# Self-attention in pairs of heads: four score matmuls in a row, four blocks of transposes, alternating value matmuls, twice the buffers

## The reference, cut to what matters

```python
q = rope(q.reshape(B, S, N_ATTN_HEADS, HEAD_DIM), positions)      # 8 heads of 64
k = rope(k.reshape(B, S, N_ATTN_HEADS, HEAD_DIM), positions)
v = v.reshape(B, S, N_ATTN_HEADS, HEAD_DIM)
attn = dilated_mixture_attention(q, k, v).reshape(B, S, ATTN_WIDTH)
...
h = h + jnp.concatenate([attn, rec], axis=-1) @ w_out[l]
h = h + memory_cross_attention(rmsnorm(h, norm_cross_g[l]), rmsnorm(memf, norm_mem_g[l]),
                               w_cq[l], w_ck[l], w_cv[l], w_co[l])
```

## Time and profile before

| | |
|---|---|
| median of three runs | 2299.41 us |
| span of the profiled execution, first to last instruction | 2294.4 us |
| TensorE busy / VectorE / ScalarE / GpSimd | 2110.9 / 984.3 / 756.1 / 738.7 us |
| mean granted TensorE clock | 0.950 |
| self-attention, first score to the output product | 1697.03 to 1787.97 us |

### The profile page before, as it was taken

One profiled execution on the slowest core, in us unless ns is written; L12 is line 12 of the kernel. 1 busy time (PEld: TensorE's weight loads), 2 busy tenths in 40 slices (PEclk: granted clock), 3 DMA queues, 4 the chain that ended last, 5 costly groups with the idle time before them and its releaser, 6 DMA issues.

```text
span 2294.4 us, 26745 instructions
## 1 busy us (share of the span) xinstructions
PE 2110.9 (92%) x9626; PEld 1668.1 (73%) x9626; DVE 984.3 (43%) x1417; ACT 756.1 (33%) x1049; POOL 738.7 (32%) x323
## 2 busy tenths in 40 slices
PE   6999999999999987688899999979589978999997
PEld 6888888888768763456788888857453656888886
DVE  6733277145436027773511111377836344221224
ACT  2422122111364134342342222445445343332332
POOL 1323233323324211232244344423330312534432
PEclk9999999999999998777999999989789998999999
DMA  7322244234212110000233232322130211323321
GB/s 300 110 101 82 83 166 154 84 119 146 73 57 81 60 50 28 10 1 21 87 94 111 91 103 89 119 63 79 57 100 1 73 37 55 111 89 93 110 83 64
DMA packets 54426, 197.21 MB, mean 86 GB/s; under 512 B 6432, under 2 KB 6992, under 8 KB 53584
## 3 DMA queue, kind: packets, MB, share of 16 engines
q1 hardware_dynamic: 45424, 162.98, 22.5%
q10 hardware_dynamic: 8928, 33.23, 4.1%
HBM read 194.09 MB, written 2.10 MB: 86 GB/s over the span
## 4 chain that ended last, share of the span: by engine, by line
PE 78%; issue 10%; DVE 7%; ACT 3%; POOL 2%; ACTq 0%; POOLq 0%; DVEq 0%; PEldq 0%
PE ps L1518 62%; POOL wlo L443 2%; PE ps L1532 2%; PE ps L1823 2%; PE ps L1832 1%; PE ps L1505 1%; PE ps L1506 1%; PE ps L1507 1%; PE ps L1753 1%; PE ps L1688 1%; PE ps L1681 1%; PE ps L1842 1%; PE ps L1741 1%; PE ps L1729 1%; DVE decay_f L1198 1%
## 5 line engine op out<-in xcount | busy, mean ns | idle before, releaser
L443 POOL TENSOR_TENSOR wlo<-raw,whi 128x1024 fp32r<-128x1024 f32 x280 | 697.5, 2503 | 1433.6 <-ACT whi L474 1433.5
L1518 PE MATMUL ps<-h_hi,whi 128*128 128x512 f32 (+1 forms) x1600 | 520.7, 364 | 13.7 <-POOL wlo L443 6.5
L1518 PE MATMUL ps<-h_lo,whi 128*128 128x512 f32 (+1 forms) x1600 | 522.0, 365 | 0.0
L1518 PE MATMUL ps<-h_hi,wlo 128*128 128x512 f32 (+1 forms) x1600 | 518.5, 363 | 0.0
L474 ACT ACTIVATE whi<-raw 128x1024 fp32r<-128x1024 f32 x280 | 289.5, 1053 | 436.2 <-PE ps L1518 346.1
L1518 PEld LDWEIGHTS ps<-h_hi,whi 128*128 128x128 f32 x1600 | 273.1, 188 | 71.9 <-issue 11.7
L1518 PEld LDWEIGHTS ps<-h_hi,wlo 128*128 128x128 f32 x1600 | 275.6, 189 | 51.2
L1518 PEld LDWEIGHTS ps<-h_lo,whi 128*128 128x128 f32 x1600 | 274.3, 188 | 47.8 <-issue 0.7
L1518 PE MATMUL ps<-g_lo,whi 128*128 128x512 f32 (+1 forms) x784 | 260.4, 369 | 0.0
L1518 PE MATMUL ps<-g_hi,whi 128*128 128x512 f32 (+1 forms) x784 | 258.4, 366 | 0.0
L1518 PE MATMUL ps<-g_hi,wlo 128*128 128x512 f32 (+1 forms) x784 | 258.4, 366 | 0.0
(11 more groups left out here) (332 smaller groups left out, 2422.0 us busy)
## 6 DMA issues: line engine op xcount, KB each, us to landing
raw<-panels SPq DMA_DIRECT2D x280, 512.0 KB, 3.5
ada_w<-ada_t ACTq DMA_DIRECT2D x54, 512.0 KB, 4.3
ada_f<-ada_p SPq DMA_DIRECT2D x9, 512.0 KB, 15.4
ada_f<-ada_t SPq DMA_DIRECT2D x9, 512.0 KB, 15.5
x_lat<-x_t SPq DMA_DIRECT2D x1, 2048.0 KB, 9.6
out<-x_lat SPq DMA_DIRECT2D x8, 256.0 KB, 2.2
cond_b<-cond SPq DMA_DIRECT2D x1, 1024.0 KB, 4.9
x_ctx<-ctx_t SPq DMA_DIRECT2D x1, 1024.0 KB, 11.6
```

Of the source, the lines that this page charges most:

```text
L443: pool.tensor_tensor(wlo[:, sl], raw[:, sl], whi[:, sl].bitcast(f32), ALU.subtract).then_inc(lo_done, 1)
L1518: ins = pe.matmul(bank(banks + b, n), wt[:, w], a[:, at_(kc, c0):at_(kc, c0) + n], start=kc == 0 and j == 0, stop=kc == n_k - 1 and j == 2)
```

## The change

The items of the self-attention are reordered. An item n is now head 2*(n div 8) + n mod 2 and query tile (n div 2) mod 4, so the two heads of a pair alternate. TensorE works in groups of four items (`GROUP`): four score matmuls in a row, then four blocks of transposes of the group before. Every second group, from the fourth on, the value matmuls of a whole pair follow, in which the two heads alternate. ScalarE's copy now lies four items behind its exponential. There are eight probability rows (the second four where `x_ctx` was) and two buffers `prob_t` of a pair each. The cross-attention becomes a function of its own with its old order; its buffers are the new ones.

The diff, cut to its core (the functions for ScalarE and VectorE of the cross-attention keep their order and are left out; `item` and the addresses are shown once):

```diff
-P_BUFS = 4
+P_BUFS = 8
 LAG = 3
+GROUP = 4
...
-        prob = at("prob", P_BUFS * LAT, R_ADA + 8 * KB)
+        prob_a = at("prob_a", P_BUFS // 2 * LAT, R_ADA + 8 * KB)
+        prob_b = at("prob_b", P_BUFS // 2 * LAT, R_XC)
...
-        prob_t = at("prob_t", 2 * LT * LAT, R_H + 32 * KB)
+        prob_t = [at("prob_t0", 2 * LT * LAT, R_H + 32 * KB), at("prob_t1", 2 * LT * LAT, R_G + 24 * KB)]
...
+        def item(A, n):
+            if A is SELF:
+                j, it, e = n // 8, n // 2 % LT, n % 2
+                return 2 * j + e, it
+            return divmod(n, LT)
...
+            def self_attention():      # ScalarE
+                for n in range(SELF["n"] + GROUP):
+                    if n < SELF["n"]:
+                        exponential(SELF, n)
+                    if n >= GROUP:
+                        m = n - GROUP
+                        if m % 8 == 0 and m >= 16:
+                            act.wait_ge(a_values, m // 4 - 2)
+                        transposed(SELF, m)
+                        if m % 8 == 5 and m > 8:
+                            merged(SELF, m // 8 - 1)
+                merged(SELF, HEADS - 1)
...
+                    if A is SELF and n % 8 == 6 and n >= 16:      # VectorE
+                        low_output(A, n // 8 - 2)
...
+            def scores(A, n):      # TensorE
+                hd, it = item(A, n)
+                j, r = (hd // 2, slice(64 * (hd % 2), 64 * (hd % 2) + 64)) if A is SELF else (hd, slice(0, P))
+                if n >= 4:
+                    pe.wait_ge(a_max if A is SELF else a_exp, A["n0"] + n - 3)
+                pe.matmul(bank(SCORE_BANKS[n % 4], A["keys"]), A["q"][r, j * LAT + it * P:j * LAT + (it + 1) * P],
+                          A["k"][r, j * A["keys"]:(j + 1) * A["keys"]], start=True, stop=True).then_inc(a_scores, 1)
+            def transposes(A, m):
+                N = A["n0"] + m
+                pe.wait_ge(a_prob, N + 1)
+                if m >= 2:
+                    pe.wait_ge(a_copied, N - 1)
+                for t in range(A["keys"] // P):
+                    ins = pe.transpose(bank(2 + m % 2, P, t * P), prob_row(N, P, t * P), ident[:, :])
+                ins.then_inc(a_trans, 1)
+            def self_attention():
+                pe.wait_ge(win2_evac, len(WIN2))
+                pe.wait_ge(rope2_done, 8)
+                def values(j):
+                    if j >= 2:
+                        pe.wait_ge(mix_ready, SELF["s0"] + j - 1)
+                    pe.wait_ge(a_copied, 8 * (j + 1))
+                    for t in range(LT):
+                        for e in range(2):
+                            r = slice(64 * e, 64 * e + 64)
+                            v = av[:, t * 512 + (2 * j + e) * DH:t * 512 + (2 * j + e + 1) * DH]
+                            ins = pe.matmul(ps[r, (4 + j % 2) * 512:(5 + j % 2) * 512], v, prob_cols(SELF, 2 * j + e)[:, t * LAT:(t + 1) * LAT],
+                                            start=t == 0, stop=t == LT - 1)
+                    ins.then_inc(a_values, 2)
+                for g in range(SELF["n"] // GROUP + 2):
+                    if g < SELF["n"] // GROUP:
+                        for n in range(GROUP * g, GROUP * (g + 1)):
+                            scores(SELF, n)
+                    if 1 <= g <= SELF["n"] // GROUP:
+                        for m in range(GROUP * (g - 1), GROUP * g):
+                            transposes(SELF, m)
+                    if g >= 3 and g % 2:
+                        values((g - 3) // 2)
```

More of the change, by code:

```diff
@@ L367, in build, with prob_row, prob_cols @@
         CROSS = attention_items(HEADS, aq, ck, cv, P, CTX, 8 * LT, 8, 16)
+        def prob_row(N, n=LAT, c0=0):
+            sl = N % P_BUFS
+            half, sl = (prob_a, sl) if sl < P_BUFS // 2 else (prob_b, sl - P_BUFS // 2)
+            return half[:, sl * LAT + c0:sl * LAT + c0 + n]
+        def prob_cols(A, hd):
+            if A is SELF:
+                buf, e = prob_t[hd // 2 % 2], hd % 2
+            else:
+                buf, e = prob_t[0], hd % 2
+            return buf[:, e * LT * LAT:(e + 1) * LT * LAT]
+        def item(A, n):
+            if A is SELF:
+                j, it, e = n // 8, n // 2 % LT, n % 2
+                return 2 * j + e, it
+            return divmod(n, LT)
         V_BANKS = {"v": (0, 2, 4, 6), "cv": (0, 2), "rv": (0, 1, 2, 3, 4, 5), "gv": (0, 1, 2, 3, 4, 5)}
@@ L813, in rg_split @@
                     act.activation(o_hi[:, (4 + c) * LAT:(5 + c) * LAT], ru[:, c * LAT:(c + 1) * LAT], ACT.Copy).then_inc(ohi_done, 1)
[L815 to L833, removed]
@@ new lines, in exponential @@
+            def exponential(A, n):
+                N = A["n0"] + n
+                sl = N % P_BUFS
+                act.wait_ge(a_max, N + 1)
+                if A is CROSS:
+                    act.wait_ge(a_trans, N - P_BUFS + 1)
+                row = prob_row(N, A["keys"])
+                src = row if A is SELF else bank(SCORE_BANKS[n % 4], A["keys"])
+                act.activation(row, src, ACT.Exp, bias=stat[:, sl:sl + 1], scale=float(A["dk"]) ** -0.5,
+                               accum_out=stat[:, P_BUFS + sl:P_BUFS + sl + 1]).then_inc(a_exp, 1)
@@ new lines, in transposed, with merged @@
+            def transposed(A, m):
+                hd, it = item(A, m)
+                kt = A["keys"] // P
+                act.wait_ge(a_trans, A["n0"] + m + 1)
+                dst = prob_cols(A, hd).rearrange("p (j i) -> p j i", j=LT)
+                act.activation(dst[:, 0:kt, it * P:(it + 1) * P], bank(2 + m % 2, kt * P).rearrange("p (j i) -> p j i", j=kt),
+                               ACT.Copy).then_inc(a_copied, 1)
+            def merged(A, c):
+                act.wait_ge(a_values, 2 * c + 2 if A is SELF else A["h0"] + c + 1)
+                act.activation(o_hi[:, c * LAT:(c + 1) * LAT], bank(4 + c % 2), ACT.Copy).then_inc(ohi_done, 1)
@@ L834, in attention, with cross_attention @@
+            def cross_attention():
+                for n in range(CROSS["n"] + LAG):
+                    if n < CROSS["n"]:
+                        exponential(CROSS, n)
                     if n >= LAG:
                         m = n - LAG
[L836 to L844, removed]
+                        hd, it = item(CROSS, m)
+                        if it == 0 and hd >= 2:
+                            act.wait_ge(a_values, CROSS["h0"] + hd - 1)
@@ L885, in _ @@
             rg_split()
-            attention(SELF)
+            self_attention()
             outputs_and_squares(P_WOUT2, norms[5])
@@ L889, in _ @@
             cross_queries()
-            attention(CROSS)
+            cross_attention()
             for c, q in enumerate(range(P_CO + 2, P_CO + 6)):
@@ L1352, in attention @@
                         sl = N % P_BUFS
-                        row = prob[:, sl * LAT:sl * LAT + A["keys"]]
+                        row = prob_row(N, A["keys"])
                         top = stat[:, sl:sl + 1]
@@ L1358, in attention @@
                         if A is SELF:
-                            it = n % LT
+                            it = item(A, n)[1]
                             link(dve.tensor_tensor_reduce(out=row, in0=bank(SCORE_BANKS[n % 4]), in1=bias_sb[:, it * LAT:(it + 1) * LAT], scale=1.0,
@@ L1371, in attention, with low_output @@
                         dve.tensor_scalar(row, row, inv, None, ALU.mult).then_inc(a_prob, 1)
[L1372 to L1382, removed]
+                    if A is SELF and n % 8 == 6 and n >= 16:
+                        low_output(A, n // 8 - 2)
+                    if A is CROSS and n % LT == LT - 1 and n >= LT:
+                        low_output(A, n // LT - 1)
+                for c in range(2 if A is SELF else HEADS - 1, HEADS):
+                    low_output(A, c)
+            def low_output(A, c):
+                dve.wait_ge(ohi_done, A["s0"] + c + 1)
+                sl = slice(c * LAT, (c + 1) * LAT)
+                dve.tensor_tensor(o_lo[:, sl], bank(4 + c % 2), o_hi[:, sl].bitcast(f32), ALU.subtract).then_inc(mix_ready, 1)
             def rg_convolution():
@@ L1824, in values @@
                     ins.then_inc(a_values, 1)
[L1826 to L1833, removed]
+                for n in range(CROSS["n"] + LAG):
+                    if n < CROSS["n"]:
+                        scores(CROSS, n)
@@ L1843, in attention @@
[L1843 to L1846, removed]
+                        transposes(CROSS, m)
+                        if m % LT == 0 and m:
+                            values(m // LT - 1)
+                values(HEADS - 1)
             def rg_products(c):
```

33 lines of the change are left out of this document (10 added, 23 removed).

## The result

| | before | change |
|---|---|---|
| median | 2298.51 us (4 runs, 2286.91 to 2303.87) | 2260.55 us (4 runs, 2252.42 to 2266.23) |
| ratio | | 0.9847, 95% interval 0.9817 to 0.9878 |
| span of the profiled execution | 2294.4 us | 2260.9 us |
| self-attention, first score to output product | 90.9 us | 65.4 us |

The two traced executions lie 33.5 us apart: 8.0 us are there when the self-attention starts (at 1688.98 us and not at 1697.03), 25.5 come in the self-attention, and none behind it (506.5 us in both). The comparison was repeated later: median 2271.13 us, ratio 0.9887, interval 0.9857 to 0.9916. That is 26 us, nearly what the self-attention gives, and a median inside the range.

A forecast was written before the change was run, and what follows sets the result against it. TensorE was taken to bound the kernel, self-attention included. With overlapping halves, groups of 5.5 and 9.25 us brought the output product from 1787.97 to 1763.7: 2299.4 - 24.3 = 2275.1 us, 80% range 2269 to 2290.

The forecast's parts named there:

- four scores: Self-attention scores on TensorE: eight instructions of alternating heads run in pairs, 2.0 us where in series 3.6.
- sixteen value instructions: Self-attention values of a pair of heads: column halves run in pairs, 3.75 us where in series 7.1.
- group without values: Self-attention, four items without value matmuls: balanced between TensorE and VectorE at 5.5 us.
- group with values: Self-attention, four items plus a pair's value matmuls: 5.5 + 3.75 = 9.25 us.
- self-attention: From the first score to the output product: the sign named a stretch of 67 us, the product starting at 1763.7.
- gain there: End of the self-attention: the output product starts at 1763.7 and not at 1787.97, 24.3 us less.
- start of the two instructions of a pair: Sign of overlap in the self-attention: score instructions start in pairs about 0.1 us apart.
- The step that failed: From trace to median: the 24.3 us at the attention's end carried over whole, what follows moving as a block.
- Columns in series: Rival, self-attention values: column halves alternate without overlap, 3.35 us more per values step, 13.4 in all, 2288.5 us; chance 0.20.
- Neither overlaps: Rival, self-attention scores and values: no halves overlap, a pair takes 20.8 us as before, about 2297.7 us; chance 0.05.
- The clock stays at 1.2 GHz: Rival, self-attention: TensorE stays at half speed, a group takes 7.8 us and values 7.1, 2302.4 us; chance 0.05.
- Alternation of columns drains the array: Rival, self-attention values: each column switch waits, 0.73 us an instruction, values 11.7 us, 2306.9 us; chance 0.05.

The follow-up runs named there:

- experiment 9: The kernel before, unchanged, traced once more for the pace of the first feed-forward part: span 2282.9 us.
- experiment 6: The change with heads in turn and both heads of a pair writing the same column half: median 2286.16 us, ratio 0.9958, self-attention 86.2 us.
- experiment 11: The kernel before, unchanged, traced once more for the pace of the first feed-forward part: span 2295.4 us.
- experiment 1: The kernel before, unchanged, profiled and timed again: median 2297.88 us, ratio 1.0008, span 2303.5 us, self-attention 92.3 us.
- experiment 7: The change with both heads of a pair writing the same column half, scores still alternating rows: ratio 0.9895, self-attention 79.0 us.
- 8: The change with each pair's values cut into two halves, one in every group between transposes: 2263.73 us, ratio to the kernel before 0.9838, self-attention 59.8 us.
- 3: The kernel before with eight probability rows in place of four and nothing else: ratio 1.0008, self-attention 92.3 us.
- 5: The change with items in their old order, so four scores in a row belong to one head: ratio 0.9921, self-attention 74.0 us.
- experiment 4: The change with a pair's value matmuls head by head, four of the even head, then four of the odd: ratio 0.9901, self-attention 72.4 us.

## Why the prediction was wrong

**The mechanism and its terms were right.** Step by step, from the trace of the change:

| term | predicted | measured |
|---|---|---|
| four scores | 2.0 us | 1.92 |
| sixteen value instructions | 3.75 us | 3.58 |
| group without values | 5.5 us | 5.46 |
| group with values | 9.25 us | 9.13 to 9.14 |
| self-attention | 66.7 us (1697.03 to 1763.7) | 65.4 |
| gain there | 24.3 us | 25.5 |
| start of the two instructions of a pair | 0.1 us apart | 0.00 to 0.01 |

**The step that failed** stands at the head of the part on the change: "I carry the difference of the attention's end over to the median, since what follows is bound by TensorE and moves as a block." What follows does move as a block: 506.5 us in both first traces. What comes before did not stay, and the prediction gave it nothing. The first feed-forward part runs at one of two paces from one execution to the next. Its 3072 product matmuls start at 80.7 us in both first traces; the last one starts at 623.4 us at the slower pace and at 613.1 at the faster, 10.3 us less. The trace of before had the slower pace and the first trace of the change the faster. Product matmuls there alternate 512 and 256 columns; groups of them from 100 to 620 us (line, operation, count, busy us, mean ns) in the first trace of before:

```profile
L1518 PE MATMUL ps<-h_lo,whi 128*128 128x512 f32 x318 | 128.2, 403 | 0.0
L1518 PE MATMUL ps<-h_hi,wlo 128*128 128x512 f32 x318 | 126.6, 398 | 0.0
```

And in experiment 9, the same kernel:

```profile
L1518 PE MATMUL ps<-h_lo,whi 128*128 128x512 f32 x318 | 124.5, 391 | 0.0
L1518 PE MATMUL ps<-h_hi,wlo 128*128 128x512 f32 x318 | 124.5, 391 | 0.0
```

The range was built from the rivals of the self-attention alone and gave nothing to this. Three runs of before within 6.3 us of each other had suggested that there was nothing to give; 23 later ones lay between 2281 and 2305 us. The 5.0 us between span and median, which stand ahead of the prediction as time around the span, were a sign: wherever the record has both, a run is 1.8 us longer than its own span (2262.72 and 2260.9, for one), so 3.2 of the 5.0 were already the difference between two executions.

Of the 38 us between the first medians, 25.5 are the self-attention, 8.0 the stretch ahead of it in the traces, and 4.5 the distance of the medians from the traced executions, of which no trace tells. The four times of the change, 2252.4 to 2266.2 us, all lie below the 2270.1 and 2270.2 us of its two executions traced at the slower pace, and three of the four of before (2297.6 to 2303.9) lie among those of its three at the slower pace (2296 to 2305). So the first medians compared executions of the change at the faster pace with mostly slower ones of before; the second comparison (26 us) and the table of spans bear this out, but the timed executions were not all profiled, so for them it is inferred. The lowest, 2252.42 us, is 7.8 us below the lowest traced one (2260.21), so the two paces are not the whole of the scatter. Nor is it excluded that a changed program meets the faster pace more often: in six of ten executions of experiment 6 against three of 18 of before, but in two of six of the change itself in its second comparison.

So the mechanism was right and the total was missed through a term that the sum left out. The second median lies inside the range; that is no better forecast, only another draw of the same scatter.

**A smaller miss of the same kind.** The kernel before varies at the half clock: its self-attention took 90.9 us in two traces and 92.3 in two, and the output product and norm behind it 76.6 us in the former and 79.1 in the latter. The change shows 65.3 to 65.4 and 76.5 to 76.6 in all four. The half clock lasted 13.7 us in the former and 20.5 in the latter. Up to 4 us of gain come so in some executions only, and not all of them reach the span: in experiment 11 all that lies behind the self-attention still takes 506.5 us, in experiment 1 it takes 510.4.

**The rivals.** *Columns in series* fell: 3.58 us against 7.01 in experiment 7. *Neither overlaps* fell, and experiment 6 gives its price as 86.2 us, not 89. *The clock stays at 1.2 GHz* fell: 1.00 from 1704 to 1755. *Alternation of columns drains the array* fell with the first. The Trainium skill's rule on weight loads ("TensorE: Matmul & The Clock Gate", Part 3, what overlaps and what doesn't) would have the value loads wait, since the row groups do not differ: the trace disagrees, with loads of 0.137 us that lie beside running matmuls of the same rows, and 3.58 us for sixteen instructions. The 3.75 us that the prediction adds to the 2.38 times of the same page does not follow from it: that figure is for three column tiles, and 7.1 / 3.75 is 1.9 times. Two column halves measured 7.01 / 3.58, 1.96 times. Part 4 of that page, on transposes and the clock, could not be put to a test here, because scores always stood among them; what the trace shows is TensorE busy for 41.9 of the 51 us from 1704 to 1755 and the clock at 1.00.

**Where the gain comes from**, by the self-attention of the experiments:

| step | self-attention |
|---|---|
| kernel before | 90.9 us |
| groups of four and buffers (6) | 86.2, 4.7 less |
| and rows alternate (7) | 79.0, 7.2 less |
| and columns alternate (the change) | 65.4, 13.6 less |
| and values in halves (8) | 59.8, 5.6 less |

Eight probability rows alone give 0 (3). The other way round, columns without rows (6 to 5) give 12.2 and then rows (5 to the change) 8.6. With the 1.5 us by which the clock treated 5 worse than 6, these are 13.7 and 7.1, and the order in which the two overlaps are added makes no difference. The 4.7 us of the first step hold some of the clock's doing, too; how much was not separated.

## What to carry to other kernels

Where a matmul fills only half the rows or half the columns of the array, pair it with one for the other half and place the two next to each other in the program: the pair then costs what one did. Partners eight instructions apart overlap only in part (5.35 against 3.58 us), so the innermost loop is the one to alternate. Once TensorE is quicker, its in-order program decides what the others wait for: work that nobody waits for, such as the value matmuls, belongs in small pieces into the gaps between steps that wait, not in one block ahead of the step that feeds VectorE. Before a range is set from one trace, look at how far executions of the same kernel lie apart, and in which stretch; a gain of a few us cannot be told from medians of four runs that vary by 14 to 17.

## What the runs showed of the hardware that was not expected

- One program, two paces. The stream of product matmuls with 512 and 256 columns in turn runs at 567 or 578 matmuls in 100 us (six of them in 1.06 or 1.04 us) for the whole of the first feed-forward part, at a clock of 1.00 in both; 11 of 14 traces had the slower pace. What sets it was not tried and stays open.
- Column halves overlap for float32 as fully as row halves, into one and the same PSUM bank: 3.58 against 7.01 us for sixteen instructions, 1.92 against 3.63 for four scores.
- That overlap reached four matmul instructions ahead and no further in experiment 4, where the first of the second half starts at 1740.54 us, with the fifth of eight. In the linear attention of before the other head's first starts at 1010.63, 0.01 after the fifth.
- Where the half clock falls differs between executions of one program: it lasted 13.7 us in two traces of before and 20.5 in two, at the start of the self-attention, worth 1.4 us there.
